# A hybrid encoder block on one core: the mixing stage reordered, its first half-tile moved into attention and two router queries into its end

## The reference

```python
h = rms_norm(x, norm1_g)
xr, gr, q, k, v, fl = split(h @ w_in)
y_lru = rg_lru(causal_depthwise_conv(xr), ...) * gelu(gr)          # recurrent group, 512 wide
y_fox = forgetting_attention(q, k, v, log_sigmoid(fl + fox_bf))    # attention group, 512 wide
x = x + concat(rms_norm(y_lru, gn_lru_g), rms_norm(y_fox, gn_fox_g)) @ w_out
h2 = rms_norm(x, norm2_g)
x = x + peer(h2, ...)     # queries h2 @ w_q, scores against 128 subkeys per half head, top 16, experts
return rms_norm(x, final_g)
```

## Time and profile before

| what | us |
|---|---|
| median of 3 runs | 2812.67 |
| their range | 2809.37 to 2816.16 |
| the profiled execution | 2814.05 |
| its span, first to last instruction | 2812.3 |
| PE busy | 2706.6 (96%) |
| DVE busy | 2306.2 (82%) |
| POOL busy | 1456.7 (52%) |
| ACT busy | 1250.8 (44%) |
| mean granted clock of TensorE | 0.983 of 2.4 GHz |

### The profile page before, as it was taken

The page is one execution under the profiler, slowest core; times in us unless marked ns, Lnnn a source line. Parts: engine busy times, 40 slices in busy tenths (PEclk is TensorE's granted clock), DMA queues, the critical chain, the costliest instruction groups (busy, mean ns, idle before and its releaser), DMA issues. The chain is left out here.

```text
span 2812.3 us, 39998 instructions
## 1 busy us (share of the span) xinstructions
PE 2706.6 (96%) x14923; PEld 2374.2 (84%) x14923; DVE 2306.2 (82%) x4081; ACT 1250.8 (44%) x2540; POOL 1456.7 (52%) x935
## 2 busy tenths in 40 slices
PE   7999899979999999999999999989999999999998
PEld 6777665459999999999999999987788888878887
DVE  3297795329989989788979797775999999999997
ACT  4244432113332222888888888862222222222222
POOL 1122320004338885566666666662666666657662
PEclk9999899989999999999999999999999999999999
DMA  4110100323238886999999999999999999999995
GB/s 119 44 38 23 60 1 23 90 68 111 63 94 312 297 296 207 358 389 378 388 380 401 380 390 396 389 378 325 382 383 383 386 388 386 386 379 379 391 384 223
DMA packets 332114, 762.66 MB, mean 271 GB/s; under 512 B 23232, under 2 KB 158400, under 8 KB 329360
## 3 DMA queue, kind: packets, MB, share of 16 engines
...
## 5 line engine op out<-in xcount | busy, mean ns | idle before, releaser
L1985 POOL DMA_INDIRECT v_rows<-in_peer_v,row_numbers x336 | 535.6, 1594 | 332.5 <-DVE y_rest L2058 189.2
L1620 PE MATMUL expert_pre<-h2T,wq_then_uT_hi 128*128 128x320 f32 x4096 | 674.1, 314 | 24.5 <-ACT wq_then_uT_hi L1654 22.2
L1734 POOL DMA_INDIRECT u_rows<-in_peer_u,row_numbers x384 | 554.0, 1443 | 246.8 <-DVE row_weights L1754 161.0
L1620 PEld LDWEIGHTS expert_pre<-h2T,wq_then_uT_hi 128*128 128x128 f32 x4096 | 613.0, 189 | 27.3 <-issue 26.9
L2115 PE MATMUL expert_out<-v_hi,w_hi 128*128 128x512 f32 x1280 | 501.2, 392 | 12.7 <-DVE w_lo L2036 12.3
L1754 DVE CUSTOM_DVE_ANT_0 u_rows<-u_rows,h_rows_kept 128x1024 f32<-128x1024 f32 x384 | 488.3, 1300 | 27.8 <-DMA u_rows<-in_peer_u,row_numbers 27.7
L2115 PE MATMUL expert_out<-v_lo,w_hi 128*128 128x512 f32 x1280 | 499.6, 390 | 0.0
L2115 PE MATMUL expert_out<-v_hi,w_lo 128*128 128x512 f32 x1280 | 499.2, 390 | 0.0
L2058 DVE SCALAR_TENSOR_TENSOR y_rest<-v_rows,row_weights,y_rest 128x1024 f32<-128x1024 f32 x256 | 326.4, 1278 | 22.0 <-DMA v_rows<-in_peer_v,row_numbers 20.7
L1620 PE MATMUL expert_pre<-h2T,wq_then_uT_lo 128*128 128x320 f32 x2048 | 343.8, 310 | 0.6 <-POOL wq_then_uT_lo L1723 0.6
L1620 PEld LDWEIGHTS expert_pre<-h2T,wq_then_uT_lo 128*128 128x128 f32 x2048 | 312.4, 189 | 1.0 <-POOL wq_then_uT_lo L1723 0.8
...
## 6 DMA issues: line engine op xcount, KB each, us to landing
wq_then_u<-in_peer_u_turned SPq DMA_DIRECT2D x128, 512.0 KB
pick_memory<-in_peer_v SPq DMA_DIRECT2D x128, 512.0 KB
pick_memory<-acts_dram SPq DMA_DIRECT2D x128, 320.0 KB
...
wq_then_u<-in_peer_wq SPq DMA_DIRECT2D x32, 512.0 KB, 4.0
w_in_columns<-in_w_in SPq DMA_DIRECT2D x20, 512.0 KB, 3.9
```

Of the source, the lines that this page charges most:

```text
L1620: last = nc.tensor.matmul(pre[:, (2 * c + half) % 4, 0:WIDTH], part[:, c % 2, k], m.h2T[:, t, k, HALVES[half]], start=n == 0, stop=n == le ...
L1734: pool.indirect_dma_start(rows[:, k % RING], None, table, bass.IndirectOffsetOnAxis(ap=m.row_of[:, f, slot:slot + 1], axis=0)).then_inc(fe ...
L1985: pool.indirect_dma_start(rows[:, k % ROW_RING], None, d.peer_v, bass.IndirectOffsetOnAxis(ap=m.row_of[:, f, slot:slot + 1], axis=0)).then ...
```

## The change

Four banks of PSUM become one tensor, `m.front`, that lives through attention, mixing and scoring: logits and square sums in attention, the two halves of a tile in mixing, queries 0 to 2 and the keys' bank in scoring.

- *Attention.* Seven of the eight products of `mix_lru(0)` are issued behind the last weighing, then the last square sums, then the eighth product.
- *Mixing.* It begins with `mix_fox(0)`. For each b: `mix_lru(b+1)`, `turn(b)`, `mix_fox(b+1)`. DVE's order becomes normalize b, add the recurrent half of b+1, `low(b)`, add the attention half of b+1. In place of a recurrent half the last tile has query 0 of the row tiles in front of its turn, and query 1 behind it. POOL splits a third weight tile, SP loads the third and fourth.
- *Scoring.* PE begins with query 2, turns the keys, makes scores 0 and 1, and goes on with query 3 and score 2.

The diff, cut; the lines on logits that only read `logit(bank)` for `logit[:, bank]` are left out:

```diff
@@ attend
-        logit = ps("logits", [P, LOGIT_BANKS, HALF])
+        logit = lambda bank: m.front[:, bank]
-        sums = ps("square_sums_ps", [P, HALF])
+        sums = m.front[:, LOGIT_BANKS]
...
+                def first_lru(products):
+                    if 0 in products:
+                        pe.wait_ge(m.w_out_in, 16)
+                        pe.wait_ge(gained, CT + 1)
+                        pe.wait_ge(logit_read, turn(FH, 0))
+                    for n in products:
+                        half, c = divmod(n, CT)
+                        last = nc.tensor.matmul(m.front[:, half], m.gateT[:, c, 0:P], m.w_out[:, c, half * HALF:(half + 1) * HALF],
+                                                start=c == 0, stop=c == CT - 1)
+                    return last
...
+                first_lru(range(2 * CT - 1))
                 pe.wait_ge(squared, SUMS)
                 square_sums(squares[:, (SUMS - 1) % 2], 2 * NT)
+                first_lru([2 * CT - 1]).then_inc(m.lru_mixed, 1)
@@ mix_out
-        out_lru = ps("out_lru", [P, 2, HALF])
-        out_fox = ps("out_fox", [P, 2, HALF])
+        out_lru, out_fox = m.front[:, 0:2], m.front[:, 2:4]
...
-                for n in range(2):
-                    pool.wait_ge(m.wq_in[n], 16)
-                    pool.tensor_copy(m.wq_hi[:, n], m.wq[:, n]).then_inc(m.wq_hi_done, 1)
+                for n in range(3):
+                    pool.wait_ge(m.wq_in[n % 2], 16 * (n // 2 + 1))
+                    if n == 2:
+                        pool.wait_ge(m.query_done, 1)
+                    pool.tensor_copy(m.wq_hi[:, n % 2], m.wq[:, n % 2]).then_inc(m.wq_hi_done, 1)
...
-                    if b in (2, 3):
...
+                    n = b - 2 if b < 4 else b - 4
+                    if b in (2, 3, NT - 2, NT - 1):
+                        if n >= 2:
+                            sp.wait_ge(m.wq_lo_done, n - 1)
+                        sp.dma_start(m.wq[:, n % 2], d.peer_wq[:, n * P:(n + 1) * P].rearrange("(k p) n -> p k n", p=P)
+                                     ).then_inc(m.wq_in[n % 2], 16)
...
-                add_groups(0)
-                add_groups(1)
+                add_lru(0)
+                add_fox(0)
                 for b in range(NT):
                     normalize(b)
+                    if b + 1 < NT:
+                        add_lru(b + 1)
                     low(b)
-                    if b + 2 < NT:
-                        add_groups(b + 2)
+                    if b + 1 < NT:
+                        add_fox(b + 1)
...
-                for b in range(2):
-                    mix_lru(b)
-                    mix_fox(b)
+                def query_of_rows(n):
+                    pe.wait_ge(m.wq_lo_done, n + 1)
+                    pe.wait_ge(dve4, max(normalizing(F - 1) + LOW, added(NT - 1, LRU_READ)))
+                    terms = [(w, part, k) for w, part in ((m.wq_hi, 0), (m.wq_hi, 1), (m.wq_lo, 0)) for k in range(KT)]
+                    for i, (w, part, k) in enumerate(terms):
+                        last = nc.tensor.matmul(m.front[:, n, 0:F * P], w[:, n % 2, k], m.h2_of_rows[:, part, k],
+                                                start=i == 0, stop=i == len(terms) - 1)
+                    last.then_inc(m.query_done, 1)
+
+                mix_fox(0)
                 for b in range(NT):
-                    if b + 2 < NT:
-                        mix_lru(b + 2)
+                    if b + 1 < NT:
+                        mix_lru(b + 1)
+                    else:
+                        query_of_rows(0)
                     turn(b)
-                    if b + 2 < NT:
-                        mix_fox(b + 2)
+                    if b + 1 < NT:
+                        mix_fox(b + 1)
+                query_of_rows(1)
@@ score
-                for s in range(2, 2 * HP):
+                for s in range(4, 2 * HP):
                     sp.wait_ge(lo_done, s - 1)
...
-                for s in range(2, 2 * HP):
+                for s in range(3, 2 * HP):
                     pool.wait_ge(hi_done, s + 1)
...
-                for n in range(HP):
+                query_of(2)
+                turn_keys()
+                score_of(0)
+                score_of(1)
+                for n in range(3, HP):
                     query_of(n)
-                    if n == 0:
-                        turn_keys()
-                    else:
-                        score_of(n - 1)
+                    score_of(n - 1)
...
+                query_out(0)
+                query_out(1)
+                split_high(3)
+                for g in range(HP // 4):
+                    act.wait_ge(keys_turned, g + 1)
+                    A(keysT[:, 4 * g:4 * g + 4, :], keys_ps, ACT.Copy).then_inc(keysT_done, 1)
+                scores_out(0)
+                query_out(2)
+                scores_out(1)
+                split_high(4)
```

58 lines of the change are left out of this document (29 added, 29 removed).

## The result

The changed kernel took 2796.86 us, the median of 4 runs (2791.54 to 2803.60), against 2814.01 us for the kernel before (4 runs, 2809.37 to 2816.16). The ratio is 0.9943 with a 95% interval of 0.9921 to 0.9966. A repeat gave 2794.72 us (8 runs, 2788.44 to 2801.36) against 2811.40 (13 runs), ratio 0.9937, 0.9916 to 0.9959. The forecast was 2793 with a range of 2787 to 2800: both medians lie inside, 2 to 4 us above it.

A forecast was written before the change was run, and what follows sets the result against it. TensorE was taken to work without a gap through mixing and scoring, except at three places where it had little to do. Terms summed to -19.65 us: 2814.05 to 2794.4 us profiled, 2793 as a median, range 2787 to 2800.

The forecast's parts named there:

- end of attention: Seven products fill TensorE's gap before the last square sums, which then run at full clock; -0.35 us.
- mixing up to the end of the last attention half: One half less -6.86, no slow start -1.46, one more turn +0.88, gain row wait +0.7; -6.75 us.
- end of mixing: Only tile 7 left to normalize, with queries 0 and 1 filling TensorE; 10.3 us instead of 14.63, -4.3 us.
- start of scoring until the keys are out: New 3.0 us wait for keys behind query 2, two turning rounds at half clock; +0.25 us.
- rest of scoring: Two queries fewer behind the keys, 2 x 4.25 us; -8.5 us.
- M to E: From the last weighing's start in attention to the expert stage's first product; all terms together, -19.65 us.
- B: End of attention: the seven products come after the squares, moved and not hidden; 8.6 us given back, 2801.6 us; chance 0.04.
- C: Scoring: DVE's picks start no earlier, so the gain is not passed on; 2805, or 2812 us; chance 0.07.
- D: Mixing loop: a chain too long to be covered makes TensorE wait in seven tiles; 2822 us at 11 us; chance 0.03.
- A: Start of scoring: clock at half through four rounds, scores 0 and 1, queries 3 and 4; 2796.5 us; chance 0.10.
- The rule against the row: Key turning: the skill's rule has transposes never at full clock, so all four rounds slow; sum 1.1 us smaller.
- the sign by which it called itself wrong: After scoring: the stretch to the end stays 1982 us; changing by several us would make the forecast wrong.

The follow-up runs named there:

- kernel without the cover: Changed kernel with the first recurrent half moved from the end of attention back to the start of mixing; 2804.18 us.
- two-bank kernel: Changed kernel with keys loaded in mixing, key turning alternating between two PSUM banks, and the gain row loaded before the second x row; 2785.34 us.
- cover alone: Kernel before with only the attention part: first recurrent half split around the last square sums, loop order and queries unmoved; 2805.32 us.
- no queries: Changed kernel with queries 0 and 1 moved from mixing back to scoring; 2802.28 us.
- keys early: Changed kernel with the subkeys' load issued in the middle of mixing instead of at the start of scoring; 2789.63 us.
- query 3 first: Changed kernel with query 3 placed before the turning of the keys; 2797.67 us.
- one pass more: Changed kernel with one extra VectorE pass per tile between attention half and normalized rows; 2798.89 us.
- three passes more: Changed kernel with three extra VectorE passes per tile between attention half and normalized rows; 2812.98 us.

## Why the prediction was right

The terms, from the two profiled executions of the first comparison:

| term | predicted | measured |
|---|---|---|
| end of attention | -0.35 | 9.99 - 10.38 = -0.39 |
| mixing up to the end of the last attention half | -6.75 | 110.07 - 116.74 = -6.67 |
| end of mixing | -4.3 | 10.24 - 14.63 = -4.39 |
| start of scoring until the keys are out | +0.25 | 13.05 - 13.16 = -0.11 |
| rest of scoring | -8.5 | 201.51 - 209.26 = -7.75 |
| M to E | -19.65 | -19.31 |

The end of the last attention half is its row's start and length in both kernels, 593.59 and 586.92; in both DVE starts its addition 0.11 us later.

**End of attention.** As worked out: fourteen records in the gap, sums at full pace, mixing 9.99 us after M.

**Loop.** No wait but the one for the gain row. PE's next half began 7.54 us after the first (476.85 to 484.39) instead of 6.86, which is the 0.7 us forecast; the 0.44 in brackets counts from a modelled end. The term came out within 0.1 us of the sum. Part of that is luck of the trace: 1.46 us of it is the slow start of the very execution that the prediction was read from, and the next execution of the same kernel lost 3.0 there. Against that one the stage gained some 1.5 us more than forecast. The spare of the loop was bracketed by the two chain experiments: 1.3 us more cost nothing there, 3.9 us more cost 1.9 in each tile.

**End of mixing.** The chain took 4.65 us (586.92 to 591.57) against the 4.6 worked out, and PE waited 0.48 us behind query 0. The turn (0.85) and query 1 with the next stage's start (4.74) came as forecast.

**Start of scoring.** The keys wait came at 2.36 us instead of 3.0: PE began to turn them 6.76 us after the stage began, not 7.3. Two rounds ran at half clock, which I had taken; the four took 6.3 us where I had put 6.1. The other two executions of the changed kernel put four and two rounds at half.

**The two queries.** The pair was right as 8.5 us of work, but "the same loss falls on scores 0 and 1 and query 3, so it is in neither sum" was off by about 0.6 us: in the first execution the two scores took 2.59 us from start to start instead of 1.36 (604.10 - 602.74 at full clock), and query 3 5.89 (612.80 to 618.69) instead of 4.25, so 2.9 us of loss against 2.3. That is most of the 0.75. The repeats lost 2.7 each; the repeat of the kernel before lost 1.7 at query 1.

**Rivals.** B is excluded by the kernel without the cover, C by DVE's first pick at 613.70, 20.5 us earlier than in the earlier trace rows, and by the stage's length, which follows PE's rows: from the keys out to E the two-bank kernel takes 198.63 us, the changed one 201.51, and 2.87 of the difference of 2.88 is the slow clock in scores 0 and 1 and query 3. DVE's spare at the end did not grow to 9 us: it is 7.89 in both kernels, since its run from the first pick to the last lengthened from 188.57 to 190.13 (613.70 to 803.83). A wait of 0.77 us at 624.91 is half of that; the other half I can't name. D was no risk: 2 us spare in every tile. A, all four rounds at half and scores behind them, happened in one of three executions of the changed kernel; it cost 1.0 us from S to E, not 3.5, since query 4 was back at full clock.

**The rule against the row.** The rounds of key turning ran at full clock in all four (cover alone, no queries, keys early, two banks), in three (query 3 first), in two (the first and third executions of the changed kernel) or in none (its repeat, and the kernel with one pass more), with the same transposes. The Trainium skill, "TensorE: Matmul & The Clock Gate", Part 4 (PE-mode transpose), would have them slow in all; the runs do not agree. Nor does the idle time in front decide it by its length, as all thirteen profiled executions show. The wait is PE's in front of the first round; a round counts as slow above 0.9 us; the loss is what the scores and the query behind the rounds took beyond full clock.

| execution | wait, us | slow rounds | loss, us |
|---|---|---|---|
| cover alone | 0 | 0 | 1.4 |
| keys in mixing | 0 | 0 | 1.6 |
| two banks | 0 | 0 | 0 |
| query 3 first | 0 | 1 | 2.1 |
| without the two queries | 0.68 | 0 | 0.1 |
| before | 0.82 | 1 | 2.3 |
| before, repeated | 1.09 | 2 | 1.7 |
| one pass more | 2.22 | 4 | 1.5 |
| changed | 2.36 | 2 | 2.9 |
| three passes more | 2.40 | 3 | 2.0 |
| changed, third time | 2.44 | 2 | 2.7 |
| without the first half in attention | 2.47 | 2 | 1.7 |
| changed, repeated | 2.62 | 4 | 2.7 |

Behind a wait of 1.1 us or less none to two rounds were slow, behind 2.2 us or more two to four. Within the second group the number does not follow the wait (four behind 2.22 us, two behind 2.47), and what sets it stays open.

**The total.** It is -19.3 us up to E but -17.15 us in medians (2796.86 - 2814.01), and -16.7 in the repeat. Of the profiled pair, only 10.5 us of span are left, since the rest of the changed kernel took 1990.1 us against 1981.7. That rest is the part which the prediction named as not covered, and 8.4 us more of it is the sign by which it called itself wrong; the profiled execution itself took 2803.60 us, outside the range. It was the slowest of its four; the forecast was for a median, and the repeats below did not show the lengthening again. PE's waits in it, from E to the end (us in total, times, longest), of before:

```profile
PE expert_pre L1620 <- ACT wq_then_uT_hi L1654: 22.2, 11, 11.0
PE expert_out L2115 <- DVE w_lo L2036: 12.3, 8, 4.6
```

and of the changed kernel:

```profile
PE expert_pre L1661 <- ACT wq_then_uT_hi L1695: 23.8, 15, 9.9
PE expert_out L2156 <- DVE w_lo L2077: 15.4, 13, 4.7
```

They are 4.7 of the 8.4 us longer. In the repeats the same two waits sum to 33.9 and 30.7 us, and to 35.8 in the repeat of the kernel before (34.5 and 39.2 in the pair above). The repeats bring the rest to 1984.2 and 1981.0, inside what the other kernels show, so no lengthening by the change is shown. Whether 2 us of it are systematic stays open: the intervals of the ratios are some 6 us to either side.
